# VectorE folds the four blocks of squares of the head outputs before one product with the ones

## The reference, cut to what matters

```python
def _rmsnorm(x, g):
    xf = x.astype(jnp.float32)
    y = xf * lax.rsqrt(jnp.mean(xf * xf, axis=-1, keepdims=True) + NORM_EPS)
    return (y * g.astype(jnp.float32)).astype(x.dtype)

def second_block(x, c, w_ada, b_ada, g_mix, w_in, g_dil_out, g_sb_out, w_out, g_ffn,
...
        o_dil = _dilated_mixture(heads_d(q_d), heads_d(k_d), heads_d(v_d)).reshape(b, s, D_DIL)
        o_sb = _stick_breaking_attention(heads_s(q_s), heads_s(k_s), heads_s(v_s)).reshape(b, s, D_SB)
        mixed = jnp.concatenate([_rmsnorm(o_dil, g_dil_out[layer]),
                                 _rmsnorm(o_sb, g_sb_out[layer])], axis=-1)
        x = x + gate_mix[:, None, :] * (mixed @ w_out[layer])

        h2 = _modulate(_rmsnorm(x, g_ffn[layer]), shift_ffn, scale_ffn).reshape(b * s, d)
        y = _hierarchical_moe(h2, w_group[layer], w_expert[layer],
                              w_gate[layer], w_up[layer], w_down[layer]).reshape(b, s, d)
```

## Time and profile before

| | before |
|---|---|
| median of 3 runs | 1089.74 us |
| the profiled execution, its own time | 1089.16 us |
| its span | 1087.3 us |
| PE busy | 995.4 us (92%) |
| DVE busy | 540.7 us (50%) |
| ACT busy | 392.6 us (36%) |
| POOL busy | 497.2 us (46%) |
| chain that ended last: PE, DMA, DVE | 69%, 22%, 5% |

### The profile page before, as it was taken

How to read it: one execution, slowest core, us unless ns; L and a number is a source line. 1 busy time by engine, 2 the same in 40 slices (tenths; PEclk the granted TensorE clock), 3 DMA queues, 4 the chain that set the end, 5 groups by cost and what they waited for, 6 DMA issues and landing times.

```text
span 1087.3 us, 16618 instructions
## 1 busy us (share of the span) xinstructions
PE 995.4 (92%) x6882; PEld 735.3 (68%) x6882; DVE 540.7 (50%) x999; ACT 392.6 (36%) x562; POOL 497.2 (46%) x211
## 2 busy tenths in 40 slices
PE   7999999999999999999899999999959787959777
PEld 7989988788788888887898895544425343424333
DVE  5999987665367776214358544333212122212115
ACT  6445545554475444546597441000000000000002
POOL 5987799879598887987666510000000000000000
PEclk9999999999999999999999999999989898989889
DMA  9754455557379999638443989999999999999996
GB/s 368 299 191 156 156 194 194 193 191 281 138 254 392 361 368 378 238 117 337 136 153 117 365 347 419 428 424 428 430 424 428 429 433 421 431 426 426 432 420 258
DMA packets 36943, 341.96 MB, mean 315 GB/s; under 512 B 4225, under 2 KB 4609, under 8 KB 6530
## 3 DMA queue, kind: packets, MB, share of 16 engines
q1 hardware_dynamic: 35424, 337.82, 77.9%
q10 hardware_dynamic: 1442, 3.05, 0.8%
HBM read 339.81 MB, written 1.05 MB: 314 GB/s over the span
## 4 chain that ended last, share of the span: by engine, by line
PE 69%; DMA 22%; DVE 5%; ACT 3%; issue 1%; POOL 0%; another core or an unknown queue 0%; DVEq 0%; SPq 0%; ACTq 0%
DMA body<-in_gu 21%; PE ps L554 16%; PE ps L556 16%; PE ps L555 16%; PE ps L1224 7%; PE ps L1266 5%; PE ps L1255 2%; PE ps L1205 1%; PE ps L757 1%; PE ps L1243 1%; ACT sph L1357 1%; PE ps L983 1%; PE ps L810 0%; PE ps L1239 0%; POOL spl L2721 0%
## 5 line engine op out<-in xcount | busy, mean ns | idle before, releaser
L2721 POOL TENSOR_TENSOR spl<-raw,sph 128x1024 fp32r<-128x1024 f32 x202 | 492.5, 2473 | 127.1 <-ACT sph L1357 126.8
L1357 ACT ACTIVATE sph<-raw 128x1024 fp32r<-128x1024 f32 x196 | 200.4, 1055 | 105.7 <-PE ps L556 90.2
L2736 POOL TENSOR_SCALAR body<-body,SM 128x512 f32<-128x512 f32 x1 | 1.6, 1566 | 447.8 <-DVE SM L1940 447.8
L1892 ACT ACTIVATE ar<-ps 64x256 f32<-64x256 f32 x32 | 12.1, 377 | 333.4 <-PE ps L1224 333.4
L554 PE MATMUL ps<-sph,xbh 128*128 128x512 f32 x304 | 119.6, 394 | 0.4 <-DVE ar L2395 0.4
L556 PE MATMUL ps<-sph,xbl 128*128 128x512 f32 x304 | 118.5, 390 | 0.0
L555 PE MATMUL ps<-spl,xbh 128*128 128x512 f32 x304 | 118.4, 389 | 0.0
L1266 PE MATMUL ps<-ar,ar 128*128 128x512 f32 x240 | 110.5, 603 | 0.0
L1985 DVE SCALAR_TENSOR_TENSOR ps<-ar,COL,ps 128x256 f32<-128x256 f32 x232 | 92.1, 484 | 0.0
L2672 DVE TENSOR_TENSOR ar<-ar,ps 64x256 f32<-64x256 f32 x32 | 13.5, 423 | 139.9 <-ACT ar L1892 139.9
L554 PE MATMUL ps<-xah,sph 128*128 128x256 f32 x288 | 82.7, 287 | 0.0
(11 more groups left out here) (358 smaller groups left out, 1805.3 us busy)
## 6 DMA issues: line engine op xcount, KB each, us to landing
raw<-in_stream SPq DMA_DIRECT2D x126, 1024.0 KB, 5.7
body<-in_gu SPq DMA_DIRECT2D x11, 4096.0 KB, 47.3
body<-in_dn SPq DMA_DIRECT2D x15, 2048.0 KB, 45.7
body<-in_gu SPq DMA_DIRECT2D x10, 2048.0 KB, 25.5
body<-in_gu SPq DMA_DIRECT2D x14, 1024.0 KB, 10.9
body<-in_dn SPq DMA_DIRECT2D x12, 1024.0 KB, 11.6
tops<-in_gu SPq DMA_DIRECT2D x6, 2048.0 KB, 39.5
tops<-in_dn SPq DMA_DIRECT2D x4, 2048.0 KB, 47.8
```

What stands on the lines that cost most here:

```text
L1357: e.activation(u.half(SPH[u.n % NSP], h), u.half(RAW[u.slot], h), ACTF.Copy).then_inc(w.up(hi_ok), 1)
L1892: e.activation(HS[x % 2][0:64, :], ps[bank_of["gu", x]][0:64, 0:256], ACTF.Silu).then_inc(w.up(hsa_ok), 1)
L2721: e.tensor_tensor(u.half(SPLO[u.n % NSP], h), u.half(RAW[u.slot], h), u.half(SPH[u.n % NSP], h), ALU.subtract).then_inc(w.up(lo_ok), 1)
```

## The change

DVE gets a step `add_squares` for each kind: it waits for both squares, adds the upper 512 columns of `OSQ[kind]` to the lower 512, and then the upper 256 of these to the lower 256, both in place and both with inputs and output in SBUF. PE's `o_sum` then makes one product with 256 columns in place of four, and waits for the second addition (`added_ok`) in place of the second square (`osq_ok`).

```diff
@@ o_sum (PE)
                 claim(b)
-                w.wait_ge(osq_ok, 3 * n + 2)
-                for k in range(4):
-                    mm = e.matmul(ps[b][:, 0:256], ones, OSQ[kind][:, 256 * k:256 * k + 256], start=(k == 0), stop=(k == 3))
-                mm.then_inc(w.up(os_mm), 1)
+                w.wait_ge(added_ok, 2 * n + 2)
+                e.matmul(ps[b][:, 0:256], ones, OSQ[kind][:, 0:256], start=True, stop=True).then_inc(w.up(os_mm), 1)
                 free[b] = [(ors_ok, 5 * n + 1)]
@@ vector (DVE)
+            def add_squares(kind, n):
+
+                s = OSQ[kind]
+                w.wait_ge(osq_ok, 3 * n + 2)
+                for c in (512, 256):
+                    own()
+                    e.tensor_tensor(s[:, 0:c], s[:, 0:c], s[:, c:2 * c], ALU.add).then_inc(w.up(added_ok), 1)
+
@@
             di_norm(1)
+            add_squares("s", 0)
             for h in range(4):
                 w.wait_ge(dt_mm, 2 * h + 2)
                 own()
                 e.tensor_copy(LT[1][:, h, :], ps[bank_of["dt", 1, h]][:, 0:384]).then_inc(w.up(od_ok), 1)
             heads_norm("s", 0, "g_sb_out_2")
+            add_squares("d", 1)
             heads_norm("d", 1, "g_dil_out_2")
```

More of the change, by code:

```diff
@@ L472, in program @@
         zero_ok = sem("zero_ok")
+        added_ok = sem("added_ok")
         rsb_mm, first_hi, first_ok, scaled_ok = sem("rsb_mm"), sem("first_hi"), sem("first_ok"), sem("scaled_ok")
```

## The result

The changed kernel takes 1095.49 us (median of 20 runs, 1094.80 to 1096.87), the one before 1089.98 us (20 runs; one of them took 1104.85, the others 1089.38 to 1091.71). The ratio is 1.0049, with a 95% interval of 1.0039 to 1.0058: it is slower by 0.5%, or 5.5 us. The profiled execution of the changed kernel took 1094.98 us with a span of 1093.2, against 1089.16 and 1087.3 before.

A forecast was written before the change was run, and what follows sets the result against it. PE's path up to the issue at 632.24 was taken to bound the kernel, a full DMA stream following. Terms +2.9 ("s"), +1.1 (clock) and +0.5 ("d") gave +4.5 us, forecast 1094.2 us, range 1091.0 to 1095.9.

The forecast's parts named there:

- the likeliest case: Whole kernel: both additions of "s" wait and the clock falls, 1094.2 us, spanning 1093.5 to 1094.8 by its clock term; 50%.
- a rival at +6.1 us: PE's clock falls for longer, or for "d" too: up to +6.1 us, 1095.9 us; 8%.
- The upper bounds of the three terms: The terms' highest values: "s" +2.9 us, lower clock 1.6, "d" +1.1 if the clock also falls briefly there.
- What bounds the kernel: PE's path up to SP's issue at 632.24, which ends a DMA hole; PE's changes before it pass on one to one.
- The stream running dry between the early issues: Near 609 us transfers may run dry for 2 us; that only shortens the hole at 630.
- The additions of "s": Near 604 us on DVE: both additions wait for POOL, copies 4.2 us late, products save 1.3: +2.9 us.
- the case for which the rows with two such instructions in a row were taken: DVE at "s": both additions wait, POOL's queued instruction running between them; first copy 4.2 us late, net +2.9 us.
- the rival with one wait: DVE at "s": only the first addition waits for POOL, +0.8 + 0.5 = +1.3 us, 1091.1 us; 10%.
- The clock: PE behind its 4.2 us idle time at "s": granted clock falls to 0.50, +1.1 us, bounds 0 and 1.6.
- The rival in which the clock stays up: PE's clock does not fall after the idle time at "s": +3.4 us, 1093.1 us; 18%.
- The additions of "d": Near 618 us: first addition waits for POOL, second does not; PE 1.8 us late, saves 1.3: +0.5 us.
- The other side: The additions lie wholly beside PE's work and both savings stay: -2.6 us, 1087.1 us; 4%.

The follow-up runs named there:

- e11_pool_memset: The changed kernel, but POOL writes zeros in place of the low parts of two units of `w_out`: 1090.02 us, ratio 0.9999 to the kernel before.
- e5_one_add: The changed kernel with only the 512-column addition per kind, PE keeping two of four products: 1091.11 us, ratio 1.0012 to the kernel before.
- e8_reduce_between: The changed kernel with one one-input reduction per kind for the two additions, that of "s" behind the second copy: 1091.28 us, ratio 1.0005.
- e1_only_s: The changed kernel with only "s" folded, "d" keeping its four products: 1094.07 us, ratio 1.0035 to the kernel before.
- e4_late_s: The changed kernel with the two additions of "s" moved behind the four copies: 1094.07 us, ratio 1.0037 to the kernel before.
- e6_filler: The changed kernel with eight products of zeros in PE's idle time ahead of the sixth turned tile: 1093.57 us, ratio 1.0031.
- e2_only_d: The changed kernel with only "d" folded, "s" keeping its four products: 1090.65 us, ratio 1.0005 to the kernel before.
- e3_reduce: The changed kernel with one one-input reduction per kind in place of the two additions, same places: 1090.94 us, ratio 1.0010.

## Why the prediction was right

**The forecast and the range.** Forecast 1094.2, measured 1095.49; slower, as given 76%. The difference between the kernels was forecast as +4.5 us and is +4.83 in the trace up to the issue, +5.5 in the medians. The 0.7 us between these two lie outside the stretch of the change, and no run here takes them apart; what is shown is that the stretch of low clock near 520 and the part behind the issue differ from one execution to the next, by 1.3 and by 2.7 us. A further 0.24 us is the median of the kernel before, 1089.98 over 20 runs where the forecast started from 1089.74. So the measured time lies above the 1094.8 that was given to the likeliest case, and that it fell inside the range is in part luck: the range's end, 1095.9, comes from a rival at +6.1 us for which no sum is shown. The upper bounds of the three terms (2.9, 1.6 and 1.1) give +5.6, or 1095.3.

**What bounds the kernel.** Right. The issue at 632.24 moved to 638.12, by the whole 5.9 us of this execution, and the 455.1 us behind it did not change. The stream running dry between the early issues cost nothing, as said: the stretch from 610.8 to 614 has a DMA share of 0.59, and what was issued late was moved before the hole. In stretches of 1 us the DMA share is under 0.2 from 629 to 633 before and from 634 to 639 now: the hole begins 5 us later and ends 6 us later, so it is not shorter but about 1 us longer.

**The additions of "s".** Right in each step. First addition: 1.5 us forecast, 1.54 measured (604.99 to 606.53); second: 2.5, measured 2.44; first copy 4.2 us late, measured 4.1 (608.05 against 603.96). `e11_pool_memset` shows POOL's subtraction as the cause, `e5_one_add` shows that the second wait is the larger one, and `e8_reduce_between` shows that it takes two inputs. So the case for which the rows with two such instructions in a row were taken held, and the rival with one wait did not. The Trainium skill's rule in "SBUF — State Buffer" (section "SBUF: two separate sides") holds here down to its limit that only a GpSimd instruction that reads SBUF counts: the memset held nothing up.

**The clock.** That it falls was right, the size was a little small: +1.1 us forecast, 1.5 measured. The mis-sized part is the moment. I had the clock fall 2.9 us after the idle time began, so that part of the low stretch met no work. The idle time began at 605.87 (609.71 - 3.84), the clock was still at 1.00 up to 610.6 and then at 0.50 from 610.8 to 614: it fell about 4.8 us after the beginning, and all of the low stretch met work. In `e1_only_s` and `e4_late_s` it fell about 3.9 and 3.8 us after. What sets the moment is not shown. The rival in which the clock stays up needed `e6_filler` to come true, and then gave +3.22 where it had +3.4.

**The additions of "d".** +0.5 forecast, +0.57 in the changed kernel and +0.42 in `e2_only_d`; PE was idle for 1.60 us, not 1.8, and the clock did not fall.

**The other side.** Even without any wait for POOL the change gives 0.85 us (`e11_pool_memset`), not the 2.6 of that rival: "s" comes out at about zero, since the copies are late by about as much as the products save, and "d" at -0.8, as the bounds of the two said (0 and -0.7).

## What to carry to other kernels

Before work is moved to an engine that looks half idle, ask who reads SBUF beside it: a DVE instruction with two SBUF inputs waits for the end of POOL's running reading instruction, and a second one right behind it waits for the next, so a chain of small additions can cost a multiple of its own time. Ask also what stands behind it on its queue: here four copies that had 0.2 us to spare held up PE. And a long idle time of PE has to be priced with the stretch of half clock that can follow it: the clock fell behind each of the three idle times of 2.60 us and more at this place, and cost another 1.5 (`e6_filler`) to 1.7 us (the estimate for `e4_late_s`).

## What the runs showed of the hardware

- A DVE reduction of 128x1024 to 128x256 in groups of four takes 1.95 us when the four lie 256 columns apart and 1.22 us when they are neighbours.
- An ACT square of 128x512 from PSUM takes 0.60 us into contiguous columns and 1.11 to 1.14 us into columns four apart.
- POOL's memset of 128x1024 (two in 1.84 us) does not hold up DVE's additions with two SBUF inputs; its subtraction does.
- Between 604 and 620 us, PE's clock fell to 1.2 GHz in the three traces with an idle time of 2.60 (`e4_late_s`), 3.84 (the changed kernel) or 3.85 us (`e1_only_s`) there. It stayed at 2.4 GHz in the ten others, whose longest idle times there were 1.78 (`e3_reduce`), 1.53 (`e8_reduce_between`) and 1.34 us (`e5_one_add`), and it stayed there behind 1.48 (`e2_only_d`) and 1.60 us (the changed kernel) ahead of the sum of "d".
- The length of one idle time does not decide it alone: near 518.5 the clock fell behind idle times of only 0.82 and 1.03 us in two of 13 traces (the changed kernel and `e4_late_s`). In the others it stayed up there and fell only in or behind the idle time that follows, 3.15 or 3.16 us. How long it stayed low there differed too, from 3.4 to about 10 us for the same work.
